# Mixer's middle: two groups of transposes cut in half around projection halves, and a value product moved behind the fifteenth projection

## The chip, the cores and the metric

The kernel runs on one core of a Trainium2 chip, in one launch. The metric is the device time of that launch in microseconds, from the first instruction to the last store.

## The reference

Two equal layers. Each has a token mixer (four branches over one wide input projection) and an expert layer; 256 tokens, width 1024. The change lies in the mixer alone, so the rest is cut here to its calls.

```python
def reference(x, ...):
    for i in range(DEPTH):                       # DEPTH = 2
        h = rmsnorm(x, norm_mix[i])
        x = x + token_mixer(h, w_in[i], ...)
        x = x + peer(rmsnorm(x, norm_ffn[i]), ...)
    return rmsnorm(x, norm_final)

def token_mixer(h, w_in, ...):
    c = split_columns(h @ w_in)                  # many column blocks of 256
    o_ret = retention(q, k, v, g, ret_norm)
    o_moba = moba(apply_rope(q), apply_rope(k), v)
    o_ssm = mamba2(z, xbc, dt, ...)
    o_nsa = nsa(apply_rope(q), k_cmp, v_cmp, k_slc, v_slc, k_win, v_win, gates, ...)
    return concatenate([o_ret, o_moba, o_ssm, o_nsa]) @ w_out

def ssd_chunked(x, dt, a, bm, cm):               # the state-space branch, one chunk of 256
    acum = cumsum(dt * a)
    decay = where(causal, exp(seg(acum)), 0)
    scores = einsum(ch, bh) * decay
    y_diag = einsum(scores, x * dt)              # "state-space values"
    ...

def nsa(...):                                    # two of its three parts
    o_w = softmax(q @ k_win + mask) @ v_win      # window: group 0
    o_s = softmax(q @ k_slc + mask) @ v_slc      # selection: group 1
    ...                                          # compressed part: an MLP on blocks of k and v
```

## The kernel before

All five engines run their own program, written out in order by hand, and meet at semaphores. Nothing is scheduled by a tool: the order of calls in the source is the order on the engine.

**Weights.** Every weight comes as a piece of 128x1024 through a ring of four slots. SyncE loads piece n when piece n-4 has been used up (`piece_done >= n-3`). A float32 product is made of three products of a faster format, so ScalarE first casts a piece to its upper part (`upper(q)` into WH, two buffers) and GpSimd subtracts that from the piece for the lower part (`low` into WL, two buffers). TensorE then multiplies 16 matmuls with WH and 8 with WL. One projection n is two such pieces; I call the halves 13a, 13b, 14a, 14b, 15a, 15b. Between them stand pieces of the compressed part's weights (`compress(m)`), which TensorE reads from the ring directly. The ring holds, in this stretch: 13a, compress 4, 13b, compress 5, 14a, compress 6, 14b, compress 7, 15a, 15b. ScalarE evacuates a whole projection with `take(n)`.

**Between the projections** stand the branches' own products. A softmax group g (0: window, 1: selection) goes: scores on TensorE, mask and maxima on VectorE, `exps(g)` on ScalarE, then `turn_group` on TensorE transposes each of 4 heads' probabilities (3 blocks of 128x128) into one of two PSUM banks, and ScalarE copies each out (`probabilities`, into PT[0] or PT[1]). With two banks, a turn may begin only when the turn two before it has been copied out. Then `values` multiplies them by the values, in bank 6.

**The state-space branch.** ScalarE takes the exponential of the whole decay tensor SEG (128x1536) once; VectorE multiplies it by the scores (L1826, which raises `ps_ready` to 2), TensorE runs `values` on it into bank 6, and VectorE adds that product to the skip term, out of bank 6 (L1835, which raises `pv_evac` to 1). Bank 6 is then free for the window's `values`, which waits for just that. VectorE's program between L1826 and L1835 is fixed: L1826, the skip term (L1829), the rotation and scaling of the retention queries (L1652, L1653, L1654, L1655, L1800), L1835. The change does not touch it, nor GpSimd's or SyncE's.

The two waits on which the steps below rest:

```python
pe.wait_ge(L.tr_evac, 8)
pe.wait_ge(L.pv_evac, 1)
values(lambda h: PT[0][:, h, :], y_values(V_WIN, 0))
```

Of the kernel before, what the change touches and what calls it, by code (L numbers as in the profile page):

```python
# [34 lines left out]
HD, NH = 64, 4  # L35
# [20 lines left out]
PROJ = [0, 1, 2, 3, 4, 5, 6, 11, 12, 13, 14, 15, 16, 17]  # L56
# [32 lines left out]
def slot_of_w1(m):  # L89

    return 2 * W1 + 2 * m + 1
# [9 lines left out]
NSA_Q, MOBA_Q, MOBA_K, MOBA_V, RET_Q, RET_K, RET_V, RET_G, SSM_Z = (256 * i for i in range(2, 11))  # L101
# [147 lines left out]
def program(nc, x_t, stream, params, consts, w_last, out_t):  # L249
    ctx = ExitStack()  # L250
    with ctx:
# [178 lines left out]
        with nc.Block() as block:  # L430
# [101 lines left out]
            def _(pe):  # L532
                for layer in range(DEPTH):
# [97 lines left out]
                    def project(n, halves=(0, 1)):  # L631
                        j = PROJ.index(n)
                        if 0 in halves:
                            if j >= 2 + N_XBC:
                                pe.wait_ge(L.evac, j - 1 - N_XBC)
                            elif j >= 2:
                                pe.wait_ge(L.conv_ready, j - 1)
                        for k in halves:
                            by_token(n, j % 2, k)
# [3 lines left out]
                    def turn(blocks):  # L643

                        k = sets[0]
                        if k >= 2:
                            pe.wait_ge(L.tr_evac, k - 1)
                        for i, b in enumerate(blocks):
                            mm = nc.tensor.transpose(bank[2 + k % 2][:, i * P:(i + 1) * P], b, ident)
                        mm.then_inc(L.tr_done, 1)  # L650
                        sets[0] += 1

                    def columns(c):
                        return [Y[:, t, c + i * P:c + (i + 1) * P] for i in range(2) for t in range(TT)]
# [19 lines left out]
                    def half(block, h):  # L674
                        return T[(h % 2) * HD:(h % 2) * HD + HD, block, :]

                    def values(weights, v, b=6):

                        for h in range(NH):
                            w, vh = weights(h), v(h)  # L680
                            nc.tensor.matmul(bank[b][:, h * HD:(h + 1) * HD], w[:, 0:P], vh[0], start=True, stop=True)
                            o = bank[b][:, 256 + h * HD:256 + (h + 1) * HD]
                            nc.tensor.matmul(o, w[:, P:2 * P], vh[0], start=True, stop=False)
                            mm = nc.tensor.matmul(o, w[:, 2 * P:3 * P], vh[1], start=False, stop=True)
                        mm.then_inc(L.pv_done, 1)

                    def y_values(c, step):
                        return lambda h: [Y[:, t, c + h * step:c + h * step + HD] for t in range(TT)]

                    def turn_group(buf, g):  # L690
                        for h in range(NH):
                            pe.wait_ge(L.exp_done, 8 * g + 2 * h + 2)
                            turn([buf[:, h, i * P:(i + 1) * P] for i in range(3)])

# [54 lines left out]
                    def compress(m):  # L749


                        i, k = m // 4, m % 4
                        if k == 0:
                            pe.wait_ge(padded, 2 * layer + 1)
                            pe.wait_ge(L.blocks_ready, i + 1)
                        w = piece(slot_of_w1(m)).rearrange("p (j m) -> p j m", j=CHUNKS // 4)
                        for j in range(CHUNKS // 4):
                            mm = nc.tensor.matmul(bank[7][32 * j:32 * j + 32, i * 256:(i + 1) * 256],
                                                  BL[:, i, CHUNKS // 4 * k + j, :], w[:, j, :],
                                                  start=(k == 0), stop=(k == 3), tile_position=(0, 32 * j))  # L760
                        mm.then_inc(L.piece_done, 1)
# [38 lines left out]
                    acr(1)  # L800
                    project(13, (0,))
                    compress(4)
                    turn_group(SC4[0], 0)
                    project(13, (1,))
                    compress(5)
                    project(14, (0,))
                    turn_group(SC4[1], 1)
                    compress(6)
                    pe.wait_ge(L.seg_ready, 4)
                    pe.wait_ge(L.ps_ready, 2)  # L810
                    values(lambda h: SEG[:, h, :], lambda h: [XDT[:, t, h * HD:(h + 1) * HD] for t in range(TT)])
                    project(14, (1,))
                    compress(7)
                    pe.wait_ge(L.tr_evac, 8)
                    pe.wait_ge(L.pv_evac, 1)
                    values(lambda h: PT[0][:, h, :], y_values(V_WIN, 0))
# [2 lines left out]
                        mm = nc.tensor.matmul(bank[7][:, 16 * i:16 * i + NCMP],  # L819
                                              HID[:, i // 2, i % 2 * P:(i % 2 + 1) * P], cn("sum4"), start=True, stop=True)  # L820
                    mm.then_inc(hid_tr, 1)
                    pe.wait_ge(L.roped, 3)
                    turn(columns(MOBA_Q))
                    turn(columns(MOBA_K))
                    project(15, (0,))
                    pe.wait_ge(L.hid_ready, 3)
                    for b in range(2):
# [329 lines left out]
            def _(act):  # L1157
# [11 lines left out]
                for layer in range(DEPTH):  # L1169
# [11 lines left out]
                    def upper(q):  # L1181

                        n = slot_of(SPLIT[q // 2], q % 2)
                        act.wait_ge(*arrival(n))
                        if q >= 2:
                            act.wait_ge(L.mix_used, q - 1)
                            act.wait_ge(L.mix_lo, q - 1)
                        elif layer > 0:
                            act.wait_ge(last.hi_used, 2 * TILES - 1 + q)
                            act.wait_ge(last.vlo_ready, TILES - 1 + q)  # L1190
                        nc.scalar.copy(WH[:, q % 2, :], ring[:, n % SLOTS, :]).then_inc(L.mix_hi, 1)  # L1191

                    def take(n, next_too=True):

                        j = PROJ.index(n)
                        if next_too:
                            upper(2 * j + 2)
                            upper(2 * j + 3)
                        if n < N_XBC:
                            return  # L1200
                        act.wait_ge(L.piece_done, slot_of(n, 1) + 1)
                        b = j % 2
                        c = 256 * Y_BLOCK[n]
                        dst = Y[:, :, c:c + 256]
                        src = bank[b].rearrange("p (k m) -> p k m", k=2)
                        factor = rs_half if n >= GATED else rs
                        for t in range(TT):
                            taken_y = nc.scalar.mul(dst[:, t, :], src[:, t, :], factor[:, t:t + 1])
                        taken_y.then_inc(L.evac, 1)
                        if n >= GATED:  # L1210
                            act.wait_ge(L.evac, j + 1 - N_XBC)
                            for t in range(TT):
                                gated = nc.scalar.activation(src[:, t, :], src[:, t, :], ACT.Tanh,
                                                             scale=rs_half[:, t:t + 1])
                            gated.then_inc(L.z_exp, 1)
# [12 lines left out]
                    def exps(g, buf, heads=range(NH)):  # L1228
                        act.wait_ge(L.negm_ready, g + 1)
                        for h in heads:  # L1230
                            for t in range(TT):
                                s = buf[:, h, 0:P] if t == 0 else buf[:, h, P:3 * P]
                                k = t * NH + h
                                nc.scalar.activation(s, s, ACT.Exp, bias=negm[g][:, k:k + 1], scale=HD ** -0.5,
                                                     accum_out=rsum[g][:, k:k + 1]).then_inc(L.exp_done, 1)

                    def probabilities(buf):
                        for h in range(NH):
                            taken(buf[:, h, :], 384).then_inc(L.tr_evac, 1)

                    def squares(t, h, added):
# [75 lines left out]
                    take(12, next_too=False)  # L1317
                    upper(2 * PROJ.index(13) + 1)
                    exps(1, SC4[1], (0, 1))
                    probabilities(PT[0])  # L1320
                    upper(2 * PROJ.index(14))
                    exps(1, SC4[1], (2, 3))
                    take(13, next_too=False)
                    act.wait_ge(L.seg_ready, 4)
                    nc.scalar.activation(SEG[:, :, :], SEG[:, :, :], ACT.Exp).then_inc(seg_exp, 1)
                    probabilities(PT[1])
                    upper(2 * PROJ.index(14) + 1)
                    upper(2 * PROJ.index(15))
                    take(14, next_too=False)
                    act.wait_ge(L.piece_done, slot_of_w1(7) + 1)  # L1330
                    nc.scalar.copy(HID[:, :, :], bank[7].rearrange("p (s n) -> p s n", s=2)).then_inc(L.hid_ready, 1)
                    upper(2 * PROJ.index(15) + 1)
                    act.wait_ge(padded, 2 * layer + 2)
                    act.wait_ge(hid_tr, layer + 1)
                    hid = bank[7][:, 0:64].rearrange("p (s b c) -> p s b c", s=2, b=2)[:, :, :, 0:NCMP]
# [918 lines left out]
```

## Time and profile before

| what | value |
|---|---|
| median of 3 runs | 1931.28 us (1931.24 to 1932.91) |
| profiled execution | 1932.08 us, of which span 1930.2 us |
| TensorE matmul busy | 1909.7 us, 99% of the span |
| VectorE / ScalarE / GpSimd busy | 67% / 52% / 65% |
| mean granted TensorE clock | 0.997 |

TensorE is nearly always busy, the others have room. A busy share says little of where the last microseconds are, so the rows below go to the stretch that the change rewrites: about 82 to 104 us of the span in the first layer, and the same 955.7 us later in the second. Times of a timeline row are its start and its length in us; a bracket is the idle time before it and what ended that.

### The profile page before, as it was taken

The numbers are of one execution on the slowest core, as the hardware profiler recorded it, in microseconds if no ns is written. First come the engines' busy times: TensorE is split into PE (matmuls) and PEld (weight loads), VectorE is DVE, ScalarE is ACT, GpSimd is POOL, SyncE is SP. The second block draws the span as 40 slices with busy tenths as digits, with TensorE's granted clock in tenths as the row PEclk, the third lists the DMA queues.
The fourth block names the chain that finished last, engine by engine and source line by source line (L and its number), as shares of the span: only waits on it lengthen the run. The fifth ranks groups of instructions, "written<-read, shape, count | busy, mean of one in ns | idle before, by whom it ended". The sixth has DMA issues, their size and how long they took to land. (4 is left out here: it accounts for less than half of the span.)

```text
span 1930.2 us, 38013 instructions
## 1 busy us (share of the span) xinstructions
PE 1909.7 (99%) x12350; PEld 1699.9 (88%) x12350; DVE 1289.6 (67%) x2922; ACT 996.0 (52%) x1581; POOL 1245.1 (65%) x626
## 2 busy tenths in 40 slices
PE   9999999999999999999999999999999999999998
PEld 9888888899999888888898888888999998888886
DVE  5656799789997444444466558996899964444444
ACT  5655444654444554455466544447544454455444
POOL 6447788877776555555574477888777765555553
PEclk9999999999999999999999999999999999999999
DMA  6525555554444566555545255555444455555553
GB/s 221 185 89 164 191 191 185 185 173 154 152 160 165 196 189 193 195 194 189 185 164 179 88 175 197 185 187 185 162 161 154 159 170 193 195 191 193 194 196 130
DMA packets 93240, 338.40 MB, mean 175 GB/s; under 512 B 10352, under 2 KB 10736, under 8 KB 93168
## 3 DMA queue, kind: packets, MB, share of 16 engines
q1 hardware_dynamic: 93168, 337.54, 52.0%
q8 instruction: 34, 0.56, 0.1%
q14 instruction: 38, 0.31, 0.1%
HBM read 336.45 MB, written 1.05 MB: 175 GB/s over the span
## 5 line engine op out<-in xcount | busy, mean ns | idle before, releaser
L491 POOL TENSOR_TENSOR WL<-ring,WH 128x1024 fp32r<-128x1024 f32 x360 | 867.7, 2413 | 342.6 <-ACT WH L1405 174.6
L1405 ACT CAST WH<-ring 128x1024 fp32r<-128x1024 f32 x512 | 538.4, 1052 | 695.5 <-PE PS L1099 329.4
L520 POOL TENSOR_TENSOR HX<-G,HX 128x256 fp32r<-128x256 f32 x256 | 371.4, 1451 | 320.9 <-ACT HX L1514 320.9
L2140 DVE TENSOR_TENSOR WL<-ring,WH 128x1024 fp32r<-128x1024 f32 x248 | 303.9, 1225 | 370.9 <-ACT WH L1405 370.9
L1099 PE MATMUL PS<-WH,HX 128*128 128x512 f32 x2048 | 506.2, 389 | 0.0
L1099 PEld LDWEIGHTS PS<-WH,HX 128*128 128x128 f32 x2048 | 384.3, 188 | 79.8
L989 PE MATMUL PS<-HX,WH 128*128 128x512 f32 x1248 | 313.2, 393 | 0.0
L1099 PE MATMUL PS<-WL,HX 128*128 128x512 f32 x1024 | 274.0, 389 | 0.0
L989 PEld LDWEIGHTS PS<-HX,WH 128*128 128x128 f32 x1248 | 224.5, 189 | 40.3
L1031 PE MATMUL PS<-HX,WH 128*128 128x256 f32 x1024 | 255.9, 288 | 0.0
L1032 PE MATMUL PS<-HX,WH 128*128 128x256 f32 x1024 | 250.6, 283 | 0.0
L1099 PEld LDWEIGHTS PS<-WL,HX 128*128 128x128 f32 x1024 | 192.2, 188 | 39.9
L1032 PEld LDWEIGHTS PS<-HX,WH 128*128 128x128 f32 x1024 | 196.0, 191 | 0.0
L1031 PEld LDWEIGHTS PS<-HX,WH 128*128 128x128 f32 x1024 | 195.5, 191 | 0.0
L981 PEld LDWEIGHTS PS<-HX,WL 128*128 128x128 f32 x1280 | 174.0, 190 | 13.3 <-POOL WL L491 1.2
L981 PE MATMUL PS<-HX,WL 128*128 128x256 f32 x1280 | 178.5, 283 | 0.0
L1191 ACT CAST WH<-ring 128x1024 fp32r<-128x1024 f32 x104 | 109.1, 1049 | 121.8 <-DMA ring<-stream 33.1
L1934 DVE TENSOR_REDUCE G<-PS 128x256 f32<-128x512 f32 x160 | 110.2, 689 | 81.9 <-PE PS L981 79.3
L1036 PE MATMUL PS<-HX,WL 128*128 128x256 f32 x1024 | 143.5, 283 | 0.0
L1036 PEld LDWEIGHTS PS<-HX,WL 128*128 128x128 f32 x1024 | 132.1, 192 | 0.0
L2084 DVE SCALAR_TENSOR_TENSOR SQ<-IOB,slotT,PS 128x256 f16<-128x256 f16 x256 | 120.6, 471 | 0.0
L2084 DVE SCALAR_TENSOR_TENSOR OH<-IOB,slotT,PS 128x256 f16<-128x256 f16 x256 | 120.2, 470 | 0.0
(262 smaller groups left out, 2084.3 us busy)
## 6 DMA issues: line engine op xcount, KB each, us to landing
ring<-stream SPq DMA_DIRECT2D x636, 512.0 KB, 3.3
X<-x_t SPq DMA_DIRECT2D x4, 256.0 KB, 4.1
out_t<-X SPq DMA_DIRECT2D x2, 512.0 KB, 2.7
CN<-consts SPq DMA_DIRECT2D x1, 851.0 KB, 9.4
WF<-last SPq DMA_DIRECT2D x1, 512.0 KB, 9.7
PR<-params SPq DMA_DIRECT2D x2, 239.0 KB, 4.4
CN<-consts SPq DMA_DIRECT2D x1, 64.0 KB, 3.2
```

Of the source, the lines that this page charges most:

```text
L491: nc.gpsimd.tensor_tensor(WL[:, b, :], ring[:, slot, :], WH[:, b, :].bitcast(F32), ALU.subtract).then_inc(done, 1)
L520: nc.gpsimd.tensor_tensor(GL[:, s, :], G[:, tile, :], GH[:, s, :].bitcast(F32), ALU.subtract).then_inc(L.gl_ready, 1)
L981: mm = nc.tensor.matmul(o[:, 0:SEQ], wl[:, c, :], HH[:, c, :], start=False, stop=(c == DC - 1), skip_group_check=True)
L989: mm = nc.tensor.matmul(o, wh[:, c, :], HX[:, :, c, :], start=(c == 0), stop=False, skip_group_check=True)
L1031: nc.tensor.matmul(o, wh[:, c, :], HH[:, c, :], start=(c == 0), stop=False)
L1032: mm = nc.tensor.matmul(o, wh[:, c, :], HL[:, c, :], start=False, stop=False)
L1036: mm = nc.tensor.matmul(o, wl[:, c, :], HH[:, c, :], start=False, stop=(c == DC - 1))
L1099: return nc.tensor.matmul(bank[2 * t + h], g[:, t * P:(t + 1) * P], w[:, h * 512:h * 512 + 512], start=begin, stop=end)
L1405: nc.scalar.copy(WH[:, b, :], ring[:, slot, :]).then_inc(L.hi_ready, 1)
L1934: return V.tensor_reduce(dst, bank[b].rearrange("p (a n) -> p n a", a=2), AX.X, ALU.add)
L2084: ins = V.scalar_tensor_tensor(out=O1[slot].rearrange("p (a n) -> p a n", a=2), in0=bc(iota1, 1, 2), scalar=slotT[:, 0, t:t + 1], in1=bc(p ...
L2140: V.tensor_tensor(WL[:, s % 2, :], ring[:, (U0 + s) % SLOTS, :], WH[:, s % 2, :].bitcast(F32), ALU.subtract).then_inc(L.vlo_ready, 1)
```

## The change

On TensorE, each `turn_group` is cut into heads (0, 1) and heads (2, 3), with a projection half between: 13b goes between the halves of group 0, and 14b between those of group 1. The state-space `values`, which stood ahead of 14b, now stands behind it, and the two turns of the block-attention queries and keys move from behind the compressed part's small transposes to ahead of the window's `values`. On ScalarE the copies are cut likewise, and the casts move: the cast for 14b, which stood behind SEG's exponential and all copies of group 1, now stands ahead of `take(13)` and of that exponential; the cast for 15b moves ahead of the copy of HID.

```diff
                     project(13, (0,))
                     compress(4)
-                    turn_group(SC4[0], 0)
+                    turn_group(SC4[0], 0, (0, 1))
                     project(13, (1,))
+                    turn_group(SC4[0], 0, (2, 3))
                     compress(5)
                     project(14, (0,))
-                    turn_group(SC4[1], 1)
+                    turn_group(SC4[1], 1, (0, 1))
                     compress(6)
+                    project(14, (1,))
+                    turn_group(SC4[1], 1, (2, 3))
                     pe.wait_ge(L.seg_ready, 4)
                     pe.wait_ge(L.ps_ready, 2)
                     values(lambda h: SEG[:, h, :], ...)
-                    project(14, (1,))
                     compress(7)
+                    pe.wait_ge(L.roped, 3)
+                    turn(columns(MOBA_Q))
+                    turn(columns(MOBA_K))
                     pe.wait_ge(L.tr_evac, 8)
                     pe.wait_ge(L.pv_evac, 1)
                     values(lambda h: PT[0][:, h, :], y_values(V_WIN, 0))
...
-                    pe.wait_ge(L.roped, 3)
-                    turn(columns(MOBA_Q))
-                    turn(columns(MOBA_K))
                     project(15, (0,))
...
                     exps(1, SC4[1], (0, 1))
-                    probabilities(PT[0])
+                    probabilities(PT[0], (0, 1))
                     upper(2 * PROJ.index(14))
                     exps(1, SC4[1], (2, 3))
+                    probabilities(PT[0], (2, 3))
+                    upper(2 * PROJ.index(14) + 1)
                     take(13, next_too=False)
                     act.wait_ge(L.seg_ready, 4)
                     nc.scalar.activation(SEG[:, :, :], SEG[:, :, :], ACT.Exp).then_inc(seg_exp, 1)
-                    probabilities(PT[1])
-                    upper(2 * PROJ.index(14) + 1)
+                    probabilities(PT[1], (0, 1))
                     upper(2 * PROJ.index(15))
                     take(14, next_too=False)
+                    probabilities(PT[1], (2, 3))
+                    upper(2 * PROJ.index(15) + 1)
                     act.wait_ge(L.piece_done, slot_of_w1(7) + 1)
                     nc.scalar.copy(HID[:, :, :], ...)
-                    upper(2 * PROJ.index(15) + 1)
```

ScalarE before, from the cast for 14a (L1191 is a cast, L1234 an exponential of group 1, L1208 `take`, L1325 SEG's exponential, L1225 a copy of turned probabilities):

```order
L1191 CAST WH<-ring 128x1024
L1234 ACTIVATE G<-G 128x128
L1234 ACTIVATE G<-G 128x256
L1234 ACTIVATE G<-G 128x128
L1234 ACTIVATE G<-G 128x256
L1208 ACTIVATE G<-PS,NS 128x256 x2
L1325 ACTIVATE G<-G 128x1536
L1225 COPY G<-PS 128x384 x4
L1191 CAST WH<-ring 128x1024 x2
L1208 ACTIVATE G<-PS,NS 128x256 x2
```

ScalarE of the change, from the same cast (its lines are 3 to 5 further down: L1194, L1237, L1211, L1330, L1228):

```order
L1194 CAST WH<-ring 128x1024
L1237 ACTIVATE G<-G 128x128
L1237 ACTIVATE G<-G 128x256
L1237 ACTIVATE G<-G 128x128
L1237 ACTIVATE G<-G 128x256
L1228 COPY G<-PS 128x384 x2
L1194 CAST WH<-ring 128x1024
L1211 ACTIVATE G<-PS,NS 128x256 x2
L1330 ACTIVATE G<-G 128x1536
L1228 COPY G<-PS 128x384 x2
L1194 CAST WH<-ring 128x1024
L1211 ACTIVATE G<-PS,NS 128x256 x2
```

The cast for 14b has come from behind SEG's exponential to two places ahead of it, and the cast for 15a and `take(14)` now have group 1's first copies alone ahead of them.

TensorE before, from the end of the state-space `values` (L684) to the start of the window's (L681); L613 is a projection half, L758 `compress`:

```order
L684 MATMUL PS<-G 128x64
L613 MATMUL PS<-WH,HX 128x256 x16
L613 MATMUL PS<-WL,HX 128x256 x8
L758 MATMUL PS<-ring,G 32x256 x4
L681 MATMUL PS<-G 128x64
```

TensorE of the change at the same place, where L649 is the two turns of the block attention:

```order
L683 MATMUL PS<-G 128x64
L684 MATMUL PS<-G 128x64
L759 MATMUL PS<-ring,G 32x256 x4
L649 MATMUL PS<-CN,G 128x128 x8
L681 MATMUL PS<-G 128x64
```

Between the two `values` that share bank 6 stood a projection half and a compress step; now a compress step and eight transposes stand there.

## Rows read from the trace of the kernel before

**Rows 1.** TensorE's waits, whole span: us in total, times, longest.

```profile
PE PS L649 <- ACT G L1225: 2.8, 6, 0.8
```

**Rows 2.** Timeline of TensorE, first layer: start, length, line, count, idle before.

```profile
82.31 0.88 PE L649 MATMUL PS<-CN,G 128*128 128x128 f32 x6
83.52 0.90 PE L649 MATMUL PS<-CN,G 128*128 128x128 f32 x6 [0.33 <-ACT G L1225]
84.17 2.16 PE L613 MATMUL PS<-WH,HX 128*128 128x256 f32 x16
...
87.79 2.18 PE L613 MATMUL PS<-WH,HX 128*128 128x256 f32 x16
89.81 1.12 PE L613 MATMUL PS<-WL,HX 128*128 128x256 f32 x8
90.77 0.82 PE L649 MATMUL PS<-CN,G 128*128 128x128 f32 x6
91.92 0.90 PE L649 MATMUL PS<-CN,G 128*128 128x128 f32 x6 [0.33 <-ACT G L1225]
92.75 0.64 PE L758 MATMUL PS<-ring,G 128*32 128x256 f32 x8
93.32 0.44 PE L681 MATMUL PS<-G 128*128 128x64 f32 x2
...
99.63 0.43 PE L681 MATMUL PS<-G 128*128 128x64 f32 x2
...
102.36 1.02 PE L819 MATMUL PS<-CN,G 128*128 128x15 f32 x8
103.22 1.07 PE L649 MATMUL PS<-CN,G 128*128 128x128 f32 x8
104.05 2.16 PE L613 MATMUL PS<-WH,HX 128*128 128x256 f32 x16
```

**Rows 3.** Timeline of ScalarE in the same stretch.

```profile
87.81 0.81 ACT L1208 ACTIVATE G<-PS,NS 128x256 f32<-128x256 f32 x2
88.52 1.48 ACT L1325 ACTIVATE G<-G 128x1536 f32<-128x1536 f32 x1
...
94.43 1.05 ACT L1191 CAST WH<-ring 128x1024 fp32r<-128x1024 f32 x1 [0.16 <-DMA ring<-stream]
```

**Rows 4.** Ring loads by their line, 60 to 100 us: from issue to landing.

```profile
DMA to landing us min/median/max: 3.1/3.7/4.8
```

**Rows 5.** Timeline of VectorE, first layer.

```profile
90.03 1.76 DVE L1826 TENSOR_TENSOR G<-G 128x1536 f32<-128x1536 f32 x1 [5.28 <-ACT G L1325]
...
93.82 0.69 DVE L1655 TENSOR_TENSOR G<-G 128x512 f32<-128x512 f32 x1
94.55 2.74 DVE L1800 TENSOR_TENSOR G<-G,CN 128x512 f32<-128x512 f32 x1
97.32 0.69 DVE L1835 TENSOR_TENSOR G<-PS,G 128x512 f32<-128x512 f32 x1
...
102.16 2.72 DVE L1800 TENSOR_TENSOR G<-G,CN 128x512 f32<-128x512 f32 x1
```

**Rows 6.** Timeline of GpSimd, first layer.

```profile
86.21 2.39 POOL L491 TENSOR_TENSOR WL<-ring,WH 128x1024 fp32r<-128x1024 f32 x1 [3.22 <-ACT WH L1191]
94.36 5.19 POOL L491 TENSOR_TENSOR WL<-ring,WH 128x1024 fp32r<-128x1024 f32 x2 [5.75 <-ACT WH L1191]
101.50 2.83 POOL L491 TENSOR_TENSOR WL<-ring,WH 128x1024 fp32r<-128x1024 f32 x1 [1.96 <-ACT WH L1191]
```

**Rows 7.** Timeline of TensorE after its longest idle time, near the start.

```profile
10.47 0.38 PE L561 MATMUL PS<-HX,WH 128*128 128x256 f32 x1 [1.76 <-ACT WH L1191]
```

**Rows 8.** TensorE by stretches: length, busy (instructions), granted clock, DMA share, GB/s.

```profile
11.75:15.25 3.50, 3.50 (x19) 0.52 1.02 421
15.25:17.00 1.75, 1.75 (x17) 0.99 0.22 84
134.00:137.40 3.40, 2.45 (x19) 1.00 0.50 154
```

More of the change, by code:

```diff
@@ L675, in half, with values @@
                         return T[(h % 2) * HD:(h % 2) * HD + HD, block, :]
-                    def values(weights, v, b=6):
-                        for h in range(NH):
+                    def values(weights, v, b=6, heads=range(NH)):
+                        for h in heads:
                             w, vh = weights(h), v(h)
@@ L684, in values, with turn_group @@
                             mm = nc.tensor.matmul(o, w[:, 2 * P:3 * P], vh[1], start=False, stop=True)
-                        mm.then_inc(L.pv_done, 1)
+                        if NH - 1 in heads:
+                            mm.then_inc(L.pv_done, 1)
                     def y_values(c, step):
                         return lambda h: [Y[:, t, c + h * step:c + h * step + HD] for t in range(TT)]
-                    def turn_group(buf, g):
-                        for h in range(NH):
+                    def turn_group(buf, g, heads=range(NH)):
+                        for h in heads:
                             pe.wait_ge(L.exp_done, 8 * g + 2 * h + 2)
@@ L1235, in exps, with probabilities @@
                                                      accum_out=rsum[g][:, k:k + 1]).then_inc(L.exp_done, 1)
-                    def probabilities(buf):
-                        for h in range(NH):
+                    def probabilities(buf, heads=range(NH)):
+                        for h in heads:
                             taken(buf[:, h, :], 384).then_inc(L.tr_evac, 1)
```

## The prediction

> **What bounds the kernel now.** I read the waits of TensorE first, then its timeline where the change lies, then the engines that it waits for. TensorE is the bound: the page gives it 99% of the span, and its waits are few. The only ones that the change is about are those on copies of turned probabilities [rows 1]: six in all, 2.8 us. Four of them are the two groups of this stretch in two layers. The timeline shows one [rows 2]: two turns from 82.31, then 0.33 us of idle time, then the other two from 83.52 to 84.17. The last two need 0.65; the first two with the wait take 1.21, so the wait costs 0.56. The same stands before 91.92. That is all the gain there is here: 4 x 0.56 = 2.2 us of 1932.
>
> The reader is then to look at what else hangs on this stretch. ScalarE takes SEG's exponential at 88.52, right behind `take(13)` at 87.81, and waits for nothing there [rows 3]. VectorE starts L1826 as that ends, at 90.03, and goes through a fixed list to L1835 at 97.32 to 98.01 [rows 5], which frees bank 6. TensorE comes for bank 6 at 99.63 [rows 2]: 1.6 us to spare.
>
> **The change part by part, first layer.**
>
> TensorE does the same matmuls, and the DMAs are the same. Cutting groups removes 2 x 0.56 = 1.12. It has a seam price: a pair of turns costs 0.65 ahead of a projection, 0.83 ahead of a compress step (91.92 to 92.75), and more pairs now stand ahead of something else than a projection. Adding up the steps in the new order (compress 0.57, pairs 0.65 and 0.83, a half followed by turns 2.98, from 87.79 to 90.77, values 2.7, the eight transposes 0.83, all from [rows 2] by start to start) I get 0.27 for that, so 0.85 is left. Without a new wait 15a would start at 104.05 - 0.85 = 103.20, and the window's `values` (102.36 - 99.63 = 2.73) with the small transposes behind them (0.86) at 99.61: as early as before. But the state-space `values` and bank 6 are used closer to it, and bank 6 has to be free by then.
>
> So I follow when L1835 ends now. 13b starts at 82.31 + 0.65 = 82.96; a half takes 2.02 + 1.12 = 3.14 to its end [rows 2], so it ends at 86.10. Piece 28, for 14b, is loaded into the slot that 13b frees. From the end of a piece's use to the cast of the piece that replaces it, 14a and the cast for 15a show 94.43 - (89.81 + 1.12) = 3.50 [rows 2, 3]; the loads' bounds are 3.1 and 4.8 from issue to landing [rows 4]. With 3.50 the cast for 14b starts at 89.60. Before, that cast stood behind them in ScalarE's order; now `take(13)` and SEG's exponential are queued behind it on ScalarE. Cast 1.05, `take(13)` 0.71, exponential 1.48: it ends at 92.84 instead of 90.00. TensorE does not feel that at once, but VectorE starts L1826 at 92.87 instead of 90.03.
>
> VectorE's own work from there: 94.55 - 90.03 = 4.52 for the first six operations, 0.73 for L1800 if it runs free like L1655 of the same size, and 0.69 for L1835 [rows 5]: 98.81. But L1800 took 2.74, not 0.69. It lay beside GpSimd's low part for 14b, from 94.36 [rows 6], and ended only after that; the second L1800 ended at 104.88, after the low part that ends at 104.33. Conversely a low part alone takes 2.39, but 5.19 for two with L1800 between them, and 2.83 where L1655 was running at its start. L1835, which reads PSUM, took its 0.69 in the middle of a low part. So an operation of VectorE with both inputs in SBUF and a low part do not run together: whichever comes second waits, and GpSimd gets in between two of VectorE's operations. One such meeting costs VectorE's list 2.74 - 0.69 = 2.05. (The Trainium skill, GPSIMD Engine Reference, section Key points, says that GpSimd shares its SBUF interfaces with VectorE and contends with instructions that have two SBUF inputs; by that rule all six operations from L1826 to L1800 are exposed, not L1800 alone, and the trace agrees with its 2.74 against 0.69.)
>
> How many low parts does the list meet now? Before: one (the low part for 15a met nothing but L1835). Now the list runs from 92.87 to 99 or later. The low part for 14b starts right behind its cast, at 90.7, and ends at 93.1: it delays L1826 by 0.2. That for 15a: 14a starts at 82.96 + 2.98 + 0.83 + 0.57 = 87.34 and ends at 90.48, landing and cast as above give 95.0, GpSimd begins at 95.1, in the midst of the list: 2.05. That for 15b: its piece replaces the one of compress 6 and has landed by then; its cast now stands behind `take(14)` (14b starts at 91.72 and ends at 94.86) and two copies, at 96.4, no longer behind the copy of HID, and ends at 97.5, which is when GpSimd is done with 15a: a third low part, begun while VectorE still has L1653 to L1800 to do: 2.05 again. L1835 ends at 98.81 + 0.2 + 4.1 = 103.1, TensorE comes for bank 6 at 99.61 and waits 3.5 us. Per layer 3.5 - 0.85 = +2.65. Queued behind that wait are the window's `values`, the small transposes and 15a; the other engines wait for those in turn, and each has over 0.9 us to spare there by the same steps, so nothing is lost twice.
>
> Nothing between is late otherwise: 14b (91.72) has its upper part at 90.65 and needs the low part 2.02 later, at 93.74, against 93.1; the second half of group 1 (94.70) needs two copies that begin as SEG's exponential ends, at 92.84; the state-space `values` (95.5) need L1826, done at 94.8. These covers are 0.6 to 1 us, and gone if piece 28 lands late; but then the bank 6 wait grows by the same, so it is the one price: bounds 3.1 and 4.8 in place of 3.5 move it by -0.4 and +1.3 per layer. I take 3.5 as the nearest row.
>
> Then the clock. TensorE's longest idle time in the trace is 1.76 us ahead of 10.47 [rows 7], and from 11.75 to 15.25 its granted clock was 0.52, the lower level of 1.2 GHz, though it was dense by then; after that 0.99 [rows 8]. In the stretch of the longest wait on copies (0.8 us [rows 1]), busy 2.45 of 3.40 [rows 8], it stayed at 1.00. A wait of 3.5 is twice the one that was followed by the fall. The price: 19 matmuls took 3.50 at the lower level where 17 take 1.75, so 3.50 - 19 x 0.103 = 1.54 at most, and nothing if the low stretch lies over the idle time itself. I take 1.2, nearer to the full price, because the stretch before lay wholly behind the idle time. (The Trainium skill, TensorE: Matmul & The Clock Gate, section Why this matters for your kernels, advises against long idle gaps between matmul bursts because the clock goes back to the lower level; by that rule the fall comes here too.)
>
> Sum: 2 x (2.65 + 1.2) = +7.7. The profiled execution's own 1932.08 becomes 1939.8; it stands 0.8 above the median of 1931.28, so I predict a median of 1939.0.
>
> **The rivals.**
> 1. *The clock holds.* The wait comes, but transposes and `values` around it keep the clock up, as around the 0.8 wait. Against it: [rows 7, 8]. 2 x 2.65: 1936.6. Chance 0.22.
> 2. *One low part instead of two* (not slower by what can be told). If VectorE, once it has the SBUF, keeps it through its list, or the low part for 15b begins only after L1800, L1835 ends at 101.05, the wait is 1.45 and a layer loses 0.6, too short a wait for the clock: 1932.5. For it: L1800 got in ahead of the second low part, which ends at 99.55. Against: the low part at 101.50 got in between L1655 and L1800 [rows 5, 6]. It decides from where the cast for 15b ends after 99.5, 2 us later than I have it. Chance 0.15.
> 3. *The change does what it says.* If the list meets no low part at all, L1835 ends at 99.0 and bank 6 is free at 99.61; or piece 28 lands so early that SEG's exponential is not held. 2 x -0.85: 1929.6. Against: the landing would have to take 2 us less than the lowest row. Chance 0.06.
>
> **How the numbers follow.** My forecast, wait and fall, has 0.55; 0.02 is left for worse. Its own range: landing -0.4 to +1.3 and clock 0 to 1.54 per layer, 1935.8 to 1942.3. The range given, 1932.3 to 1941.0, reaches into rival 2 and leaves out rival 3 and the latest landings. A change of 0.2%, 3.9 us, is about what a measurement of this kernel can tell from none: 1927.4 to 1935.1 is "same". Faster 0.02, same 0.22 (rivals 2 and 3 and some), slower 0.76.
>
> **What would show it.** Right: the four 0.33 waits on copies are gone, the two others stay; in their place two waits of about 3.5 us of the window's `values` on L1835, new in the list; ScalarE idle about 1 us on the ring ahead of the cast for 14b; SEG's exponential about 2.8 us later; two of VectorE's list stretched by some 2 us; a slice of lower clock after each wait. Wrong: if L1835 ends within 1.6 us of TensorE's arrival, I have the meetings with GpSimd wrong; if SEG's exponential is not late, the landing.

## The result, and the profile after

The changed kernel takes 1948.98 us (median of 4 runs, 1946.93 to 1949.81), the kernel before on the same chips 1931.94: ratio 1.0086, 95% interval 1.0072 to 1.0100, slower by 17.0 us. I had predicted 1939.0 and a range up to 1941.0. The direction and the mechanism are as forecast; the size is not, and two thirds of the miss lie in one term, the clock.

Waits of TensorE in the changed kernel, whole span (us in total, times, longest), which answer to [rows 1]:

```profile
PE PS L681 <- DVE G L1840: 7.6, 2, 3.9
PE PS L649 <- ACT G L1228: 1.5, 2, 0.8
PE PS L613 <- ACT WH L1194: 0.5, 1, 0.5
PE PS L613 <- POOL WL L491: 0.3, 1, 0.3
```

The six waits on copies are two: the four of 0.33 us are gone. In their place stands the wait of the window's `values` on the addition out of bank 6 (L1835 before, L1840 now), once a layer. The last two rows are 14b in the second layer, waiting for its upper and its lower part.

The three engines behind that wait, first layer (the last row of ScalarE is the cast for 14b in the second), ScalarE, VectorE and GpSimd in this order, against [rows 3], [rows 5] and [rows 6] (start, length, line; the whole kernel runs 0.42 us later than before at this point):

```profile
89.88 1.05 ACT L1194 CAST WH<-ring 128x1024 fp32r<-128x1024 f32 x1 [0.54 <-DMA ring<-stream]
...
91.56 1.48 ACT L1330 ACTIVATE G<-G 128x1536 f32<-128x1536 f32 x1
...
96.92 1.07 ACT L1194 CAST WH<-ring 128x1024 fp32r<-128x1024 f32 x1
...
1054.33 1.04 ACT L1194 CAST WH<-ring 128x1024 fp32r<-128x1024 f32 x1 [2.25 <-DMA ring<-stream]
```

```profile
93.07 1.94 DVE L1831 TENSOR_TENSOR G<-G 128x1536 f32<-128x1536 f32 x1 [7.43 <-ACT G L1330]
...
96.26 2.58 DVE L1658 TENSOR_TENSOR G<-G,CN 128x256 f32<-128x256 f32 x1
98.76 2.57 DVE L1659 TENSOR_TENSOR G<-G,CN 128x256 f32<-128x256 f32 x1
...
102.82 0.69 DVE L1840 TENSOR_TENSOR G<-PS,G 128x512 f32<-128x512 f32 x1
...
104.03 0.42 DVE L1658 TENSOR_TENSOR G<-G,CN 128x256 f32<-128x256 f32 x1
```

```profile
91.01 2.39 POOL L491 TENSOR_TENSOR WL<-ring,WH 128x1024 fp32r<-128x1024 f32 x1 [1.70 <-ACT WH L1194]
95.64 5.41 POOL L491 TENSOR_TENSOR WL<-ring,WH 128x1024 fp32r<-128x1024 f32 x2 [2.25 <-ACT WH L1194]
```

The chain is the one that was forecast. The cast for 14b waits for its piece (0.54 us on the ring), SEG's exponential ends at 93.04 and not at 90.00, and VectorE's list begins there. It meets two low parts: L1658 and L1659 take 2.58 and 2.57 us, where L1658 takes 0.42 us when GpSimd is idle (row of 104.03). GpSimd's two low parts take 5.41 us together, not 2 x 2.39. The addition ends at 103.51; less the 0.42 us of the later start this is 103.09, and I had 103.1. (The Trainium skill, SBUF — State Buffer, section Who interferes with whom, says that a VectorE instruction with two SBUF inputs contends with a GpSimd instruction that reads SBUF, and calls the ports that the two share an exclusive lock. The trace agrees: L1659, 0.42 us long by itself, ends at 101.33, 0.28 behind the second low part's end at 101.05.)

What follows on TensorE, first layer and then second, against [rows 2]:

```profile
82.73 0.88 PE L649 MATMUL PS<-CN,G 128*128 128x128 f32 x6
...
103.66 0.66 PE L681 MATMUL PS<-G 128*128 128x64 f32 x2 [3.72 <-DVE G L1840]
...
108.80 1.83 PE L825 MATMUL PS<-CN,G 128*128 128x15 f32 x8
110.47 3.43 PE L613 MATMUL PS<-WH,HX 128*128 128x256 f32 x16
113.74 1.12 PE L613 MATMUL PS<-WL,HX 128*128 128x256 f32 x8
114.69 0.53 PE L831 MATMUL PS<-G,PR 128*128 128x32 f32 x4
...
1045.62 0.88 PE L649 MATMUL PS<-CN,G 128*128 128x128 f32 x6
...
1068.00 0.41 PE L681 MATMUL PS<-G 128*128 128x64 f32 x2 [3.92 <-DVE G L1840]
...
1072.15 1.83 PE L825 MATMUL PS<-CN,G 128*128 128x15 f32 x8
1073.83 3.76 PE L613 MATMUL PS<-WH,HX 128*128 128x256 f32 x16
1077.39 1.91 PE L613 MATMUL PS<-WL,HX 128*128 128x256 f32 x8
1079.09 0.64 PE L831 MATMUL PS<-G,PR 128*128 128x32 f32 x4
```

And TensorE by stretches around those waits (length, busy and instructions, granted clock, DMA share, GB/s), against [rows 8]:

```profile
99.94:103.10 3.16, 0.00 (x0) 1.00 0.51 166
103.10:113.30 10.20, 9.64 (x45) 0.50 0.01 2
113.30:117.00 3.70, 3.26 (x29) 0.99 0.25 71
1069.00:1079.20 10.20, 10.20 (x51) 0.50 0.01 2
```

The reader is to see that the engine is idle while its granted clock still reads 1.00, and that the lower level (1.2 GHz) then lies over 10.2 us, almost all of it work, not over 3.5 as near the start. In the first layer the window's `values` take 108.80 - 103.66 = 5.14 us where [rows 2] have 2.73, the small transposes 1.67 where they had 0.86, and the upper part of 15a 3.27 where it had 2.00 (the rows of the kernel before are just below): 2.41 + 0.81 + 1.27 = 4.49. In the second layer the fall comes later, during the `values`, and reaches into the lower part of 15a: 1.42 + 0.82 + 1.56 + 0.74 = 4.54.

The end of 15a on TensorE in the kernel before:

```profile
106.05 1.12 PE L613 MATMUL PS<-WL,HX 128*128 128x256 f32 x8
107.01 0.53 PE L828 MATMUL PS<-G,PR 128*128 128x32 f32 x4
```

Where the time went, from the first turn of group 0 to the end of 15a (before: 82.31 to 107.01, 24.70 us in each layer; after: 31.96 and 33.47):

| us | layer 1 | layer 2 | forecast per layer |
|---|---|---|---|
| wait for bank 6 | 3.72 | 3.92 | 3.5 |
| waits of 14b | 0 | 0.84 | 0 |
| lower clock | 4.49 | 4.54 | 1.2 |
| gain of the halved groups (the rest) | -0.95 | -0.53 | -0.85 |
| sum | 7.26 | 8.77 | 3.85 |

7.26 + 8.77 and the 0.42 us of the start make 16.45; the spans differ by 1946.7 - 1930.2 = 16.5. The row of the gain is a remainder, and holds what a wait costs beyond its idle time: in the second layer, from the compress step to the turns behind it (1054.25 to 1058.97), 14b takes 4.72 us in place of 3.54 (91.36 to 94.90 in the first), which is 1.18 for 0.84 of idle time.

### The profile page after: what moved, and what is told of

Its sections match the earlier page's. It is cut to its first block and busy times, and to the rows that moved or that the text cites. A ratio compares the mean times of both kernels' runs of the same rounds, so it can differ in the third digit from the quotient of the medians.

```text
span 1946.7 us, 38013 instructions
## 1 busy us (share of the span) xinstructions
PE 1918.4 (99%) x12350; PEld 1709.0 (88%) x12350; DVE 1290.7 (66%) x2922; ACT 995.9 (51%) x1581; POOL 1244.4 (64%) x626
## 5 line engine op out<-in xcount | busy, mean ns | idle before, releaser
L1194 ACT CAST WH<-ring 128x1024 fp32r<-128x1024 f32 x104 | 109.1, 1049 | 129.0 <-DMA ring<-stream 33.6
## 6 DMA issues: line engine op xcount, KB each, us to landing
WF<-last SPq DMA_DIRECT2D x1, 512.0 KB, 10.1
```

## The experiments

Theories at this point. **Mine**: VectorE's list comes too late, because SEG's exponential stands behind the cast for 14b and because two operations meet low parts; TensorE idles; the idle time brings the lower clock. **Rivals**: the clock falls for another reason than the idle time (the thin products that now stand together); or VectorE is late by its load alone, without the meetings; or one of the change's other edits costs the time.

### Idle time filled

The changed kernel, with TensorE multiplying ones into a free bank in place of waiting:

```diff
+                    pe.wait_ge(L.sc_evac, 10)
+                    spin(bank[4][:, 0:P], 18)
                     pe.wait_ge(L.tr_evac, 8)
                     pe.wait_ge(L.pv_evac, 1)
```

> The changed kernel, with 18 matmuls of ones into a score bank that is free there, ahead of TensorE's wait for bank 6: nothing that they write is read, and TensorE is busy (some 3.3 us) instead of idle. Idle-time theory: the low clock of 10.2 us in each layer follows from the 3.7 to 3.9 us of idle time, so it goes, and with it 2.4 us on the window's values, 0.8 on the small transposes and 1.3 to 1.7 on 15a: about 9 us in all, 1940. Rival: the low clock follows from the thin matmuls around (transposes, 64-column values), and stays: 1949. In both, L1840 ends as late as before, 3.7 us behind TensorE's arrival.

1940.32 us, ratio to the kernel before 1.0040 (1.0025 to 1.0054). TensorE by stretches, the first with the added products in it:

```profile
98.00:105.00 7.00, 7.00 (x67) 1.00 0.20 76
105.00:115.00 10.00, 9.36 (x78) 1.00 0.17 54
```

With the same time lost in the same place but no idle time, the thin products and transposes behind it run at the upper level. So the idle time causes the fall, and the fall is worth 1948.98 - 1940.32 = 8.7 us, near the 4.49 + 4.54 = 9.03 of the table. What is left over the kernel before is mainly the wait itself, less the gain.

The same profile has a wait that no fall followed, ahead of the second layer's first projection:

```profile
972.45 0.36 PE L561 MATMUL PS<-HX,WH 128*128 128x256 f32 x1 [1.84 <-DVE HX L1611]
```

```profile
970.00:980.00 10.00, 8.16 (x69) 1.00 0.18 57
```

An idle time of 1.84 us behind 10 us of dense work left the clock at 1.00 here. The runs below have shorter ones with a fall.

### The wait alone, in the kernel before

Copies on VectorE ahead of the addition out of bank 6 in the kernel before, 4 and 7 of them; nothing else is changed, so the casts, groups and `values` stand as before:

```diff
+                    for _ in range(7):
+                        step(V.tensor_copy(TB[:, 1536:2048], bank[4]))
                     dve.wait_ge(L.pv_done, 1)
                     V.tensor_tensor(ya, bank[6].rearrange(...), ...)
```

> The same with 7 copies: 5.0 us later, a wait of 3.4 us in each layer, which is the wait of the changed kernel without any of its edits. Idle-time theory (the whole loss is the wait and the clock behind it): +6.8 for the waits and about +9 for the clock, 1948. Rival (the new order of TensorE's work has a price of its own): 1939 to 1942.

> The kernel before, unchanged on TensorE, ScalarE and GpSimd; VectorE copies one score bank 4 times to a spare buffer ahead of L1835, 0.72 us each, so bank 6 is free 2.9 us later, near 100.9, and TensorE waits 1.3 us ahead of the window's values in each layer. If a wait of that size leaves the clock at full speed: +2.6, 1934.7. If it too lowers the clock, as the 1.7 us of the run with 15b's cast moved did: 1940 to 1944.

Seven copies: 1949.10 us, 1.0088 (1.0072 to 1.0103), with this wait row, and this stretch behind the first of the waits:

```profile
PE PS L681 <- DVE G L1837: 7.0, 2, 3.5
```

```profile
103.80:114.00 10.20, 10.18 (x50) 0.53 0.01 4
```

A wait of 3.5 us at this place, with none of the change's edits, gives the change's whole loss. Seen from here the edits cost time by when bank 6 comes free; what else they do (the halved groups' gain, the waits of 14b) is small beside it.

Four copies: 1937.27, 1.0033 (1.0020 to 1.0046), but the five runs stand at two values, 1937.2 and 1942 to 1943. The profiled one is of the upper. TensorE by stretches behind its two waits:

```profile
103.00:109.80 6.80, 6.80 (x37) 0.54 0.11 42
1062.40:1072.50 10.10, 10.10 (x51) 0.51 0.15 61
```

Here waits of 1.47 and 1.72 us were each followed by the lower level, for 6.8 and 10.1 us. The lower value lies between the two times that I had named. Whether a run there has one fall or none is not known: there is no profile of one.

### One low part fewer

The changed kernel with the cast for 15b back behind the copy of HID:

```diff
-                    upper(2 * PROJ.index(15) + 1)
                     act.wait_ge(L.piece_done, slot_of_w1(7) + 1)
                     nc.scalar.copy(HID[:, :, :], ...)
+                    upper(2 * PROJ.index(15) + 1)
```

> The changed kernel, with the cast for 15b put back behind the copy of HID. Meeting theory: the low part for 15b then comes some 3 us later, behind L1805; VectorE's list meets one low part less, L1840 ends some 2.4 us earlier, near 101.1 of the first layer, and the wait is about 1.3 us in place of 3.7; if that is too short for the clock to fall, 1933, and if any wait there lowers the clock, 1943. Rival (the lateness is all from the cast for 14b and the load): the wait stays at 3.7 and the time at 1949.

1940.08 us, 1.0043 (1.0026 to 1.0060). VectorE, first layer, then TensorE's wait, then its stretch behind it:

```profile
94.53 2.72 DVE L1657 TENSOR_TENSOR G<-G,CN 128x512 f32<-128x512 f32 x1
...
99.40 0.69 DVE L1840 TENSOR_TENSOR G<-PS,G 128x512 f32<-128x512 f32 x1
```

```profile
100.24 0.41 PE L681 MATMUL PS<-G 128*128 128x64 f32 x2 [1.58 <-DVE G L1840]
```

```profile
102.60:109.40 6.80, 6.80 (x34) 0.51 0.01 2
```

The low part for 15b begins at 99.31, so the list meets one, not two, and the wait is 1.58 and 1.79 us in place of 3.72 and 3.92: one meeting is worth 2.1 us. This is my rival 2 made real, and it shows what was wrong with it: I called its wait of 1.45 "too short a wait for the clock", but behind 1.58 us the lower level came, for 6.8 us from about 102.7 on. The time fell between the 1933 and the 1943 that I had named, since the lower level lay over 6.8 us in each layer and not over 10.2.

### SEG's exponential first

The changed kernel with `take(13)` and SEG's exponential ahead of the cast for 14b:

```diff
-                    upper(2 * PROJ.index(14) + 1)
                     take(13, next_too=False)
                     act.wait_ge(L.seg_ready, 4)
                     nc.scalar.activation(SEG[:, :, :], SEG[:, :, :], ACT.Exp).then_inc(seg_exp, 1)
+                    upper(2 * PROJ.index(14) + 1)
```

> The changed kernel, with the cast for 14b put back behind SEG's exponential (ahead of group 1's first copies). Load theory: what makes L1840 late is that the exponential waits for the ring; it starts 2.2 us earlier now, the wait falls to some 1.5 us, the clock holds: 1934. Meeting theory: the list from L1831 to L1840 then runs into the low part for 14b, which it escaped, and into the other two as well; L1840 ends near 103 all the same, and 14b waits for its low part besides (up to 0.9 us): 1947 to 1950.

1943.17 us, 1.0054 (1.0037 to 1.0070). VectorE, first layer:

```profile
91.30 1.76 DVE L1831 TENSOR_TENSOR G<-G 128x1536 f32<-128x1536 f32 x1 [5.67 <-ACT G L1329]
92.97 2.87 DVE L1834 TENSOR_TENSOR G<-G,PR 128x512 f32<-128x512 f32 x1
95.88 2.75 DVE L1657 TENSOR_TENSOR G<-G,CN 128x512 f32<-128x512 f32 x1
...
99.33 2.80 DVE L1660 TENSOR_TENSOR G<-G 128x512 f32<-128x512 f32 x1
...
102.89 0.69 DVE L1840 TENSOR_TENSOR G<-PS,G 128x512 f32<-128x512 f32 x1
```

The list begins 1.8 us earlier and ends at 103.58, as late as in the changed kernel, since it now meets three low parts. A list that is late by its load would have ended earlier; the meetings decide. TensorE's wait is shorter, 2.28, mainly because 14b now waits too (1.22 us in the first layer). The median is under both this theory's 1947 to 1950 and the profiled run's 1946.42: the four runs go from 1941.28 to 1946.42. In the profiled one the lower level lies over 10.2 us in the first layer and over 6.8 in the second, so the length of the low stretch was again what I had not forecast.

### Other work ahead of the wait

The changed kernel with the small transposes and 15a ahead of the window's `values`; and then 15b ahead of the block attention's scores as well (the diff shows the first step):

```diff
-                    pe.wait_ge(L.tr_evac, 8)
-                    pe.wait_ge(L.pv_evac, 1)
-                    values(lambda h: PT[0][:, h, :], y_values(V_WIN, 0))
...
                     project(15, (0,))
+                    pe.wait_ge(L.tr_evac, 8)
+                    pe.wait_ge(L.pv_evac, 1)
+                    values(lambda h: PT[0][:, h, :], y_values(V_WIN, 0))
```

> The changed kernel, with the compressed part's small transposes and 15a ahead of the window's values, so that TensorE has 3.9 us of work between its arrival and the moment that bank 6 is free. If all the loss is that one wait and the clock behind it, nothing is left of it and the 0.85 us per layer of the forecast's gain shows: 1930.2, 1.7 below the kernel before. If VectorE's lateness hurts later stages too (the next evacuations of bank 6, the block attention's scores), 1933 or more.

> The changed kernel with the small transposes and 15a ahead of the window's values (as in the run before), and 15b ahead of the block attention's scores too, so that VectorE has a projection half's time for the late evacuation of the window's values. If the 2.0 us wait at the scores was the rest of the loss, no wait is left that the kernel before has not, the clock holds, and the 0.85 us per layer shows: 1930.4 (1.7 below before). If VectorE's lateness only moves on to the state of the next stage: 1934 or more.

15a alone: 1936.94, 1.0024 (1.0013 to 1.0036). The wait for bank 6 is gone, and the next of VectorE's results is late, the mask that the block attention's scores wait for:

```profile
PE PS L666 <- DVE G L1675: 4.1, 2, 2.1
```

The clock falls behind it too (0.51 from 108.6 to 115.3). With 15b ahead as well: 1931.24, 0.9999 (0.9990 to 1.0008), with no wait of over 1 us in this stretch and no fall. Each projection half covers one late result of VectorE's. What the halved groups gain does not show in this order's time; in its profile 14b waits 1.24 us in the second layer.

### The addition first

The changed kernel, with the rotation of the retention queries behind the addition out of bank 6 in VectorE's program:

```diff
-                    dve.wait_ge(L.roped, 3)
-                    dve.wait_ge(L.evac, 7)
-                    step(rope_ret(0))
                     dve.wait_ge(L.pv_done, 1)
                     V.tensor_tensor(ya, bank[6].rearrange(...), ...)
+                    dve.wait_ge(L.roped, 3)
+                    dve.wait_ge(L.evac, 7)
+                    step(rope_ret(0))
```

> The changed kernel, with VectorE's rotation of the retention queries put behind L1840 (the add that frees bank 6) instead of ahead of it. Meeting theory: L1840 then has only L1831 and L1834 ahead of it and ends near 99, ahead of TensorE's arrival: no wait for bank 6, the clock holds, and what is left is some lateness at the scores (0.2 to 1.5 us per layer, since the rotation still meets GpSimd): 1931 to 1934. If the add is late by something else (the load, the exponential), the wait stays above 1.5 us and the time above 1938.

1928.86 us, 0.9987 (0.9978 to 0.9996): faster than both kernels, than the one before by 3.0 us, which is just clear of noise, and below the 1931 to 1934 that I had named: the lateness at the scores did not come. VectorE, first layer (the addition is L1837 here):

```profile
96.99 0.69 DVE L1837 TENSOR_TENSOR G<-PS,G 128x512 f32<-128x512 f32 x1 [2.71 <-PE PS L684]
97.60 1.77 DVE L1657 TENSOR_TENSOR G<-G,CN 128x512 f32<-128x512 f32 x1
```

The five operations that could meet low parts now stand behind the one for which TensorE waits. Bank 6 is free at 97.68, TensorE comes at 98.3, and 81 to 110 us has a granted clock of 1.00.

The same reordering alone, in the kernel before:

> The kernel before, with one edit of VectorE's order: the addition out of bank 6 stands ahead of the rotation of the retention queries, as in the run that beat both kernels; no turn group is halved. Theory (that run's gain comes from the turn waits that the change removes, and VectorE's order only takes the new wait away): here bank 6 is free earlier, but nobody waited for it, so the time is that of before, 1931.9 within 1 us, and the six waits on copies of turned probabilities stay at 2.8 us in all. Rival (VectorE's order gains by itself, for instance by other meetings with GpSimd's low parts further down): 1929 to 1930, with no change in those six waits.

1930.72, 0.9997 (0.9988 to 1.0006): no difference. From the first turn of group 0 to the end of 15a this run takes 24.69 and 24.70 us in the two layers, as the kernel before does. The changed kernel with the addition first takes 23.49 and 23.57 (first layer, 81.27 to 104.76):

```profile
81.27 0.88 PE L649 MATMUL PS<-CN,G 128*128 128x128 f32 x6
...
104.76 0.53 PE L831 MATMUL PS<-G,PR 128*128 128x32 f32 x4
```

So the gain is that of the halved groups, 1.2 and 1.1 us a layer, and VectorE's order only removes the wait that they bring.

### Group 0 alone

The kernel before with group 0 alone halved around 13b, no cast and no value product moved:

```diff
-                    turn_group(SC4[0], 0)
+                    turn_group(SC4[0], 0, (0, 1))
                     project(13, (1,))
+                    turn_group(SC4[0], 0, (2, 3))
...
-                    probabilities(PT[0])
+                    probabilities(PT[0], (0, 1))
                     upper(2 * PROJ.index(14))
                     exps(1, SC4[1], (2, 3))
+                    probabilities(PT[0], (2, 3))
```

> The kernel before, with the turns of group 0 alone cut in half around 13b, its copies cut likewise on ScalarE; no cast, no value product and no block-attention turn is moved. Theory: two waits of 0.33 (one a layer) go, bank 6 is free as early as before, no new wait and no low clock: 2 x 0.56 less a seam of 0.1 to 0.2 a layer, 0.7 to 0.9 us off 1931.9, so 1931.0 to 1931.3, which this measurement can hardly tell from no change. Rival (any halving of turns around a projection brings a wait of the bank-6 kind): 1935 or more.

1943.38 us, 1.0062 (1.0048 to 1.0076). My expectation was wrong by 12 us, and the rival's words fit. VectorE, first layer:

```profile
90.76 1.76 DVE L1828 TENSOR_TENSOR G<-G 128x1536 f32<-128x1536 f32 x1 [6.17 <-ACT G L1327]
...
93.77 2.58 DVE L1655 TENSOR_TENSOR G<-G,CN 128x256 f32<-128x256 f32 x1
96.28 2.62 DVE L1656 TENSOR_TENSOR G<-G,CN 128x256 f32<-128x256 f32 x1
...
100.39 0.69 DVE L1837 TENSOR_TENSOR G<-PS,G 128x512 f32<-128x512 f32 x1
```

Two copies now stand between the exponentials of group 1 and SEG's, so the list begins at 90.76, not 90.03; and with group 1's last turns 0.7 us earlier (91.24, not 91.92) their copies, the cast for 14b behind those, and so the first low part come earlier too: it begins at 93.68, not 94.36. In the kernel before that low part meets L1800, the last operation that it can hold [rows 5]; here it meets L1655, three operations earlier in the list, and the next low part gets in as well. The addition ends at 101.08 instead of 98.01, TensorE waits 2.21 us, and the clock falls. The 1.6 us to spare that I read from the kernel before were less than one more meeting.

With the addition first here too:

> The kernel before with the turns of group 0 alone halved around 13b, as in the run that came out at 1943.4, and VectorE's addition out of bank 6 ahead of the rotation of the retention queries. Theory (in that run a shift of 0.7 us put two of VectorE's operations between L1654 and the addition against GpSimd's low parts, and bank 6 came 2.2 us late; nothing else was lost): with the addition ahead of the rotation no operation that a low part can hold stands before it but L1828 and L1831, bank 6 is free by 95, no wait of the window's values, no low clock, and the halving gives what was expected of it at first: 1930.0 to 1931.0. Rival (the halved group 0 loses time in another way, by its copies on ScalarE or by the loads): over 1935, with a wait elsewhere.

1929.92, 0.9994 (0.9985 to 1.0003). The wait and the lower clock are gone, and the time is 1.1 us under the kernel before's 1931.05 on the same chip: about the 0.7 to 0.9 that halving one group was to give, though by itself not to be told from no change.

## Why the prediction was right or wrong

- **The turn waits**: right. Four waits of 0.33 are gone, two others stay. (The one before 91.92 costs 1.15 - 0.65 = 0.50, not the 0.56 of the other.) The gain of 0.85 per layer was too small: without the new wait and the lower clock (the run with the addition first) it is 1.21 and 1.13, so the seam price of 0.27 did not show. In the table of the changed kernel, where it is a remainder, it is 0.95 and 0.53. Rival 3, the change without its new wait, was priced at 1929.6, and the run with the addition first gave 1928.86.
- **ScalarE's order**: right. SEG's exponential ends at 93.04 - 0.42 = 92.62, forecast 92.84.
- **The meetings**: right in number and price, two at 2.16 us each (2.58 - 0.42), forecast 2.05, shown by taking one away and by moving the list. Load alone is refuted by the run with SEG's exponential first. (From L1826 to L1800 the list has seven operations with two SBUF inputs, not the six that I counted.)
- **The wait**: 3.72 and 3.92, forecast 3.5. From the end of 13b to the cast for 14b it took 3.40 us in the first layer (86.48 to 89.88), forecast 3.50, but 4.95 in the second (1049.38 to 1054.33). There the cover of 14b that I had named at 0.6 to 1 us gave way, and TensorE waited 0.84 us for 14b, so that it came later to bank 6 and that wait grew by 0.20 alone. The layer as a whole took 8.77 - 7.26 = 1.51 us more than the first, for a cast 1.6 us later than the first layer's steps put it: the late piece is paid once, as I had said, but most of it at 14b.
- **The clock**: this step failed. The fall came, as forecast, and as the idle time's doing (the filled run). But "nothing if the low stretch lies over the idle time itself ... I take 1.2", with 1.54 "at most", took both the length of the low stretch (3.5 us) and the work in it from one stretch near the start. There it lay over a dense projection and was short. Here it lay over 10.2 us, in the first layer two thirds of them thin `values` and transposes, and cost 4.49 and 4.54: 2 x (4.5 - 1.2) = 6.6 of the 10 us by which I was off. Of the rest, 0.6 is the two waits, 0.84 those of 14b, 0.2 the gain as the table has it, 0.4 the start, and 1.2 lies between executions and medians: I took off 0.8 because the profiled execution of the kernel before stood that much above its median, and the changed kernel's stands 0.44 below its own (1948.54 against 1948.98). That the clock would fall was right for a wait of this size (both layers here, and both with seven copies), but the row that I read it from is weaker than I took it: near the start every profile has a wait of 1.66 to 2.63 us, and in five of the thirteen (1.68 to 2.18 us) the clock stayed at 1.00.
- **Rival 2**: its wait was right when its condition was made true (1.58 against 1.45), its "too short a wait for the clock" wrong in both layers of that run. My range leaned on it at the lower end, and took 1.54 as the clock's upper bound at the other.

What stays open: why the lower level lasts 6.8 us in some stretches and 10.2 in others (behind waits of 3.5 us and more it was 10.2 in every profile, behind shorter ones either), and what decides, for waits of 1.5 to 2.2 us, whether the clock falls at all.

## What to carry to other kernels

When a wait of TensorE is forecast, price the clock by the work that stands right behind the wait, and not by a low stretch seen elsewhere: in the changed kernel each microsecond of waiting cost more than one in lower clock behind it, and in other runs 1.5 us of waiting could be enough, though 1.84 us were not. On VectorE, an operation whose result frees a bank goes ahead of operations with two SBUF inputs that GpSimd can hold up; slack in front of such a bank counts only if it is larger than one more meeting. Halving a group, or an edit that shifts work by 0.7 us as the halved group 0 did, can change which operations meet, so the list has to be laid against GpSimd's for the new times.

## What the runs showed of the hardware that was not expected

- Idle times of 1.47 to 3.92 us of TensorE in this stretch were followed by a granted clock of 0.5 over 6.8 or 10.2 us. It began between 0.6 us before the end of the idle time (the changed kernel, first layer) and 2.5 us behind it (one low part fewer), so part of the work behind a wait can still run at the upper level. Waits of that size are not always followed by it: 1.84 us in the middle of the filled run were not, nor were those near the start of five runs (1.68, 1.71, 1.80, 1.88 and 2.18 us).
- The small operations pay the same for a meeting as large ones: 0.42 us became 2.58 (128x256), 0.69 became 2.87 (128x512).
- A kernel can have two times without any edit between its runs: 1937.2 and 1942 to 1943 for the one with four copies, whose waits (1.47 and 1.72 us) are the shortest that were followed by the lower clock.
